# A decoder layer on one core: SwiGLU gate and up products as seven block products, the down product in a stage of its own

## The chip, the cores and the metric

The kernel runs on one core of one Trainium2 chip. The metric is the device time of one execution in microseconds (us). Engines are called as in the profile: PE (TensorE), with PEld its weight loads, DVE (VectorE), ACT (ScalarE), POOL (GpSimd), SP (SyncE, which only issues DMAs here).

## The reference, cut to what matters

One layer of a decoder: 1024 tokens of width 1024, float32. Two gated mixers, a cross attention to 256 memory tokens, and a SwiGLU feed-forward of width 2816, each with a normalisation ahead and a residual add behind. The part in question is the last:

```python
def _swiglu(n, w_gate, w_up, w_down):
    return (jax.nn.silu(n @ w_gate) * (n @ w_up)) @ w_down
...
        h = h + _swiglu(_rmsnorm(h, g_ffn[l]), w_ffn_gate[l], w_ffn_up[l], w_ffn_down[l])
    return _rmsnorm(h, g_final)
```

## The kernel before

Activations lie transposed: features on the 128 partitions, 1024 tokens along a row, so a tensor of width 1024 is eight tiles of 128x1024. Every large product is done in three passes over float32 values that are split in a rounded part ("hi") and the rest ("lo"): hi by hi, lo by hi, hi by lo. One matmul takes a 128x128 block of weights and 512 tokens (a "half"); all these come from one line, L387 in `passes`.

Weights come as a stream of 276 tiles of 128x1024 (512 KB) in `weights`. SP loads them in turn into the two buffers of `stage` (L338); POOL makes `w_hi` (L350, two instructions of 128x512) and `w_lo` (L355, four of 128x256) in `split`; PE waits for `w_split` and tells with `w_begun` that it has begun a tile. A tile's buffers are written again when PE has begun the tile after it.

The stages at the end of the kernel, in PE's order:

- The output product of the cross attention ("OM", W_OM on): four weight tiles, each with four banks of PSUM of 12 matmuls. DVE adds each bank to the residual `h` (`add_product`, L1410). As soon as a tile of `h` has both halves, `next_operand` runs on ACT (n_hi = h times gain L1028, square L1031) and on DVE (n_lo L1417, sum of squares into `rms` L1421).
- Feed-forward, gate and up (`wide`): for each of 22 feature tiles a gate tile and an up tile, two halves each, 8 blocks of K by 3 passes = 24 matmuls in a bank. The operands are `n_hi` and `n_lo`, whose mean square goes through PE (`mean`, L408) during the first tile. DVE reads a bank and multiplies by `rms` (`half_out`, L1508), ACT applies Silu (L1081), DVE multiplies gate by up (L1516), ACT rounds (`a_hi`, L1083) and DVE takes the rest (`a_lo`, L1518).
- Down (`down`): for each pair of feature tiles, 16 banks of 6 matmuls on `a_hi` and `a_lo`. It is worked inside the loop, behind the first gate tile of the next pair, 11 pairs in all; the last pair stands behind the loop (`last_down`). DVE adds every bank to `h`.
- The tail: final normalisation (ACT L1108 squares, POOL L368 sums, DVE L1550 scales) and the stores.

Order and waits are written by hand: each engine has its own program, with loops (`Fori`), and waits on semaphores.

The tensors `stage`, `w_hi`, `w_lo`, `n_hi`, `n_lo` stand first in on-chip memory, each a multiple of 8 KB long per partition. Behind them stand some small ones (`gain` 160 bytes, `rope_c` and `r_col` 8, `stat` 112), and behind those all others, such as `m_hi`, `qm_hi`, `a_hi`.

## Time and profile before

| | |
|---|---|
| median of 3 runs | 1899.01 us (1897.57 to 1899.85) |
| the profiled execution | 1899.36 us, of which the span of the trace 1897.6 us |
| granted TensorE clock, mean | 0.975 of full speed |
| busy: PE / DVE / POOL / ACT | 94% / 52% / 37% / 33% of the span |
| instructions | 24569, of them 8610 matmuls |

Busy time counts overlapping matmuls, so a busy PE is no proof of PE at its best pace; the distance between the starts of matmuls is the better measure. The feed-forward lies in the last 750 us.

### The profile page before, as it was taken

How to read it: one execution, taken by the hardware profiler on the slowest of the kernel's cores; microseconds unless marked ns; L12 is line 12 of the kernel's file. 1: busy time of each engine (PE TensorE's matmuls, PEld its weight loads, DVE VectorE, ACT ScalarE, POOL GpSimd, SP SyncE). 2: the span in 40 equal slices, each digit the busy share in tenths (PEclk: the TensorE clock that was granted, in tenths of full speed). 3: DMA queues.
4: the chain of work that ended last, by engine and by line, in shares of the span. 5: the costliest groups of instructions: out<-in, count | busy, mean ns of one | idle time of the engine just before them, and what ended most of it. 6: DMA issues, size and time to landing. Idle time of an engine off the chain costs nothing.

```text
span 1897.6 us, 24569 instructions
## 1 busy us (share of the span) xinstructions
PE 1782.4 (94%) x8610; PEld 1446.1 (76%) x8610; DVE 994.6 (52%) x1490; ACT 629.1 (33%) x1009; POOL 709.6 (37%) x848
## 2 busy tenths in 40 slices
PE   3799999999999999789999899999999999999996
PEld 3677777777778777668887777888888888888884
DVE  7446894688469757865434553332332333333236
ACT  4215773576367557743113332000000000000003
POOL 5632223132313122134553034444434434443435
PEclk8899999999999999889999999999999999999998
DMA  5311112112111211263212011111111111111112
GB/s 191 123 46 46 31 51 64 46 39 66 49 46 38 77 40 50 90 221 133 78 55 78 12 34 45 52 48 44 44 55 44 45 55 44 44 49 50 44 44 89
DMA packets 42201, 118.59 MB, mean 62 GB/s; under 512 B 5136, under 2 KB 13584, under 8 KB 42000
## 3 DMA queue, kind: packets, MB, share of 16 engines
q1 hardware_dynamic: 21312, 75.66, 11.8%
q10 hardware_dynamic: 20816, 41.95, 6.7%
q8 instruction: 46, 0.75, 0.2%
q14 instruction: 27, 0.22, 0.0%
HBM read 97.67 MB, written 18.87 MB: 61 GB/s over the span
## 4 chain that ended last, share of the span: by engine, by line
PE 83%; DVE 7%; ACT 3%; issue 3%; DVEq 0%; ACTq 0%; POOL 0%; DMA 0%; POOLq 0%
PE ps L387 70%; PE ps L533 4%; PE ps L496 3%; PE ps L510 3%; DVE e_row L1310 1%; DVE e_row L1307 1%; DVE pt L1340 1%; DVE h L1550 1%; DVE rows L1319 1%; ACT n_hi L1028 1%; PE ps L529 1%; DVE rms L1421 1%; DVE h L1410 0%; ACT p_m L1054 0%; PE ps L663 0%
## 5 line engine op out<-in xcount | busy, mean ns | idle before, releaser
L350 POOL TENSOR_SCALAR w_hi<-w_stage 128x512 fp32r<-128x512 f32 x276 | 200.9, 745 | 1159.3 <-issue 622.5
L355 POOL TENSOR_TENSOR w_lo<-w_stage,w_hi 128x256 fp32r<-128x256 f32 x552 | 487.4, 913 | 11.5
L387 PE MATMUL ps<-n_hi,w_hi 128*128 128x512 f32 x1536 | 395.2, 398 | 11.0 <-DVE n_lo L1260 7.0
L387 PE MATMUL ps<-n_lo,w_hi 128*128 128x512 f32 x1536 | 386.2, 392 | 0.0
L387 PE MATMUL ps<-n_hi,w_lo 128*128 128x512 f32 x1536 | 385.7, 391 | 0.0
L387 PEld LDWEIGHTS ps<-n_hi,w_hi 128*128 128x128 f32 x1536 | 288.1, 190 | 74.0 <-issue 12.0
L387 PEld LDWEIGHTS ps<-n_lo,w_hi 128*128 128x128 f32 x1536 | 287.3, 188 | 59.8 <-issue 0.2
L387 PEld LDWEIGHTS ps<-n_hi,w_lo 128*128 128x128 f32 x1536 | 286.0, 188 | 58.6
L1410 DVE TENSOR_TENSOR h<-ps,h 128x512 f32<-128x512 f32 (+1 forms) x192 | 132.1, 691 | 160.0 <-PE ps L387 160.0
L1083 ACT ACTIVATE a_hi<-u_f 128x1024 fp32r<-128x1024 f32 x22 | 23.4, 1065 | 466.3 <-DVE u_f L1516 466.3
L1508 DVE TENSOR_TENSOR u_f<-ps,rms 128x512 f32<-128x512 f32 x44 | 30.4, 692 | 205.3 <-PE ps L387 205.3
L910 ACT ACTIVATE pt<-ps 128x256 fp32r<-128x256 f32 (+3 forms) x96 | 77.9, 811 | 134.0 <-PE ps L510 133.9
L1340 DVE TENSOR_TENSOR pt<-ps,pt 128x256 fp32r<-128x256 f32 (+3 forms) x96 | 91.9, 957 | 49.7 <-ACT pt L910 45.6
L387 PE MATMUL ps<-a_hi,w_hi 128*128 128x512 f32 x352 | 111.3, 395 | 1.7 <-DVE a_lo L1518 1.7
L387 PE MATMUL ps<-a_hi,w_lo 128*128 128x512 f32 x352 | 111.7, 396 | 0.0
L387 PE MATMUL ps<-a_lo,w_hi 128*128 128x512 f32 x352 | 111.5, 396 | 0.0
L1217 DVE TENSOR_TENSOR raw<-ps,rms 128x512 f32<-128x512 f32 x80 | 54.8, 685 | 92.5 <-PE ps L387 92.5
L1508 DVE TENSOR_TENSOR g_f<-ps,rms 128x512 f32<-128x512 f32 x44 | 30.3, 691 | 123.1 <-PE ps L387 120.9
L1081 ACT ACTIVATE g_f<-g_f 128x1024 f32<-128x1024 f32 x22 | 23.3, 1061 | 177.8 <-DVE g_f L1508 177.7
L510 PE MATMUL ps<-ident,rows 128*128 128x128 f32 x576 | 81.4, 279 | 0.0
L387 PEld LDWEIGHTS ps<-a_hi,w_hi 128*128 128x128 f32 x352 | 66.1, 188 | 18.8 <-DVE a_lo L1518 2.1
L387 PEld LDWEIGHTS ps<-a_hi,w_lo 128*128 128x128 f32 x352 | 66.1, 188 | 16.2
(175 smaller groups left out, 2212.2 us busy)
## 6 DMA issues: line engine op xcount, KB each, us to landing
w_stage<-weights_in SPq DMA_DIRECT2D x138, 512.0 KB, 3.3
gates_scratch<-raw ACTq DMA_DIRECT2D x16, 512.0 KB, 2.8
o_scratch<-o_sum ACTq DMA_DIRECT2D x64, 64.0 KB, 2.1
n_lo<-o_scratch ACTq DMA_DIRECT2D x8, 512.0 KB, 3.8
g_a<-gates_scratch ACTq DMA_DIRECT2D x8, 512.0 KB, 3.7
g_b<-gates_scratch ACTq DMA_DIRECT2D x8, 512.0 KB, 4.5
h<-x_t_in ACTq DMA_DIRECT2D x8, 512.0 KB, 7.5
out_t<-h ACTq DMA_DIRECT2D x16, 256.0 KB, 2.1
```

The source lines that it names most:

```text
L350: ins = pool.tensor_scalar(w_hi[:, b, at], stage[:, b, at], 1.0, 1.0, ALU.mult, ALU.mult)
L355: ins = pool.tensor_tensor(w_lo[:, b, at], stage[:, b, at], w_hi[:, b, at].bitcast(F32), ALU.subtract)
L387: ins = pe.matmul(bank, w[:, b, c:c + P], mv(k), start=(first and n == 0), stop=(last and n == total - 1))
L496: ins = pe.matmul(ps[:, 2 + h, 0:width(s)], a[hs, blk(qb)], b[hs, at], start=(n == 0), stop=(n == 2 and not diagonal))
L510: ins = pe.transpose(ps_t[:, h, n, :], rows[:, s % 4, h, blk(n)], ident[:])
L533: ins = pe.matmul(ps[:, r, blk(h, 2 * P)], v_of[m][:, c + kb, h, :, :].rearrange("p a d -> p (a d)"), pt[:, h, kb, :, :].rearrange("p a q ...
L910: act.activation(pt[:, :, 0:n, 0, :], ps_t[:, :, 0:n, :], ACT.Copy).then_inc(pt_hi_s, 1)
L1083: act.activation(a_hi[:, f, :], u_f[:, f, :], ACT.Copy).then_inc(a_hi_s, 1)
L1217: dve.tensor_tensor(raw[:, RAW[name], blk(half, HALF)], ps[:, half, :], rms[:, blk(half, HALF)], ALU.mult).then_inc(bank_free, 1)
L1340: dve.tensor_tensor(pt[:, :, 0:n, 1, :], ps_t[:, :, 0:n, :], pt[:, :, 0:n, 0, :].bitcast(F32), ALU.subtract).then_inc(pt_lo_s, 1)
L1410: dve.tensor_tensor(hj, ps[:, bank + half, :], hj, ALU.add).then_inc(bank_free, 1)
L1508: dve.tensor_tensor(dst[:, blk(half, HALF)], ps[:, bank + half, :], rms[:, blk(half, HALF)], ALU.mult).then_inc(bank_free, 1)
```

## The change

The gate and up products are taken in 2x2 blocks: the token halves and the halves of K (features 0 to 3 and 4 to 7 of eight) on the side of the activations (A11, A12, A21, A22), the halves of K and two feature tiles on the side of the weights (B11 to B22). Seven products of blocks, with four sums on each side (S1 to S4, T1 to T4) and sums of results, stand in place of the eight. A "group" is the gate or the up product of two feature tiles; there are 22 groups, each 7 products of 12 matmuls.

- The left operands (seven, with hi and lo for four blocks of K) are made once, during OM: DVE makes the sums from `h`, ACT rounds, DVE takes the rest. The first two blocks of K lie in `n_hi` and `n_lo`, so do A11 and A22 of the fourth; the others lie in new tensors `left_2`, `left_a`, `left_b` at the far end. All of this is now in pieces of 128x512, four steps n of OM, one for each weight tile.
- The right operands: DVE makes T1 to T4 for the next group, ACT rounds all seven into a ring of four slots (in place of POOL), POOL takes only the rest (two instructions of 128x256 each).
- PE leaves banks open: a bank is read by ACT (`snapshot`) after one product and PE goes on adding to it. DVE puts the four blocks of the result together from snapshots and banks.
- The hidden tiles (gate times up) are stored to memory by SP, 1 MB for a pair, and loaded again in the down stage, where they are split by ACT and DVE in `n_hi` and `n_lo`. Down's 11 pairs follow one another at the end.

The core of the diff:

```diff
+LEFT = {"A11": 0, "S1": 1, "S2": 2, "S4": 3, "S3": 4, "A12": 5, "A22": 6}
+SPLIT_AS = ("A22", "S1", "A11", "S2", "S3", "A12", "S4")
+RIGHT = ("B11", "T1", "T2", "B22", "T3", "B21", "T4")
+SLOT = (0, 1, 2, 3, 0, 1, 2)
+MADE = {"T3": 1, "T1": 2, "T2": 3, "T4": 4}
+GROUPS = 2 * FPAIRS
...
+        def left(name, k):
+            r = LEFT[name]
+            if k < 2:
+                return n_hi[:, r, blk(k, HALF)], n_lo[:, r, blk(k, HALF)]
+            if k == 2:
+                return left_2[:, r, 0, :], left_2[:, r, 1, :]
+            if name in ("A11", "A22"):
+                at = blk(name == "A22", HALF)
+                return n_hi[:, KT - 1, at], n_lo[:, KT - 1, at]
+            t, r = (left_a, int(name[1]) - 1) if name in ("S1", "S2", "S3") else (left_b, int(name == "S4"))
+            return t[:, r, 0, :], t[:, r, 1, :]
...
+            for g in range(GROUPS):
+                tile = W_FF + 2 * g
+                split_before = W_FF + 7 * (g - 1)
+                sp.wait_ge(w_split, split_before + 4 if g else W_FF - 1)
+                sp.dma_start(stage[:, 0, 0:HALF], weights[tile][:, 0:HALF]).then_inc(b11_in, 16)
+                if g == 0:
+                    sp.dma_start(stage[:, 0, HALF:], weights[tile][:, HALF:]).then_inc(b21_in, 16)
+                    sp.wait_ge(w_split, W_FF)
+                sp.dma_start(stage[:, 1, :], weights[tile + 1]).then_inc(f2_in, 16)
+                if g % 2 and g > 1:
+                    store_hidden(g // 2 - 1)
+                if g:
+                    sp.wait_ge(w_split, split_before + 6)
+                    sp.wait_ge(t_made, 4 * g)
+                    sp.dma_start(stage[:, 0, HALF:], weights[tile][:, HALF:]).then_inc(b21_in, 16)
+            sp.wait_ge(w_begun, W_DOWN - 7 + 3)
+            load_hidden(0)
+            sp.wait_ge(t_made, 4 * GROUPS)
+            load_down(0)
+            load_down(1)
...
+            with pool.Fori(0, GROUPS) as g:
+                for pos, name in enumerate(RIGHT):
+                    b, c = ring(pos)
+                    pool.wait_ge(w_rounded, g * 7 + (W_FF + pos + 1))
+                    for part in range(2):
+                        at = slice(c + part * 2 * P, c + (part + 1) * 2 * P)
+                        ins = pool.tensor_tensor(w_lo[:, b, at], right(name)[:, blk(part, 2 * P)],
+                                                 w_hi[:, b, at].bitcast(F32), ALU.subtract)
+                    ins.then_inc(w_split, 1)
...
+            def seven(g, up, first=False):
+                y, z, x = (3, 4, 5) if up else (0, 1, 2)
+                for pos, (bank, opening, closing) in enumerate((
+                        (y, True, False), (z, True, False), (y, False, False), (z, False, True),
+                        (y, False, False), (x, True, True), (y, False, True))):
+                    name = ("A11", "S1", "S2", "S4", "S3", "A12", "A22")[pos]
+                    b, c = ring(pos)
+                    pe.wait_ge(w_split, g * 7 + (W_FF + pos + 1))
+                    if pos == 0 and not first:
+                        pe.wait_ge(c_read, g * 3 - 3)
+                    if pos in (2, 3, 4, 6):
+                        pe.wait_ge(snapped, g * 4 + {2: 1, 3: 2, 4: 3, 6: 4}[pos])
+                    for p, w in enumerate((w_hi, w_hi, w_lo)):
+                        for k in range(4):
+                            if first and not up and k in (0, 3) and p < 2:
+                                made = 7 * k + SPLIT_AS.index(name) + 1 if k else 21
+                                pe.wait_ge((nhi_ready, nlo_ready)[p], 2 * KT + made)
+                            ins = pe.matmul(ps[:, bank, :], w[:, b, c + k * P:c + (k + 1) * P], left(name, k)[p == 1],
+                                            start=(opening and p == 0 and k == 0), stop=(closing and p == 2 and k == 3), skip_group_check=True)
+                            if p == 0 and k == 0:
+                                ins.then_inc(w_begun, 1)
+                    ins.then_inc(prod, 1)
...
+            for p in range(2):
+                pe.wait_ge(a_lo_s, 2 * p + 2)
+                down(W_DOWN + 2 * p, p, B_FF + 2 * KT * p, p == 0)
...
+            def right_hi(g, pos, first=False):
+                name = RIGHT[pos]
+                if first and pos < 4:
+                    act.wait_ge(w_begun, W_FF + pos // 2)
+                elif pos < 3:
+                    act.wait_ge(w_begun, g * 7 + (W_FF - 7 + pos + 4 + 2))
+                elif pos == 3:
+                    act.wait_ge(w_begun, g * 7 + (W_FF - 7 + 3 + 2))
+                else:
+                    act.wait_ge(w_begun, g * 7 + (W_FF + pos - 4 + 2))
...
+                act.activation(w_hi[:, b, c:c + HALF], right(name), ACT.Copy).then_inc(w_rounded, 1)
...
+            def group(g, up, first=False, ending=False):
+                begun = first and not up
+                snapshot(g, up, 0, 0, begun)
+                right_hi(g, 4)
+                snapshot(g, up, 1, 1)
+                right_hi(g, 5)
+                snapshot(g, up, 2, 2)
+                right_hi(g, 6)
+                snapshot(g, up, 3, 4)
+                if ending:
+                    return
+                right_hi(g + 1, 0)
+                if begun:
+                    factors(3)
+                    act.preload_act_table(ACT.Silu)
+                right_hi(g + 1, 1)
+                if not up:
+                    silu(g, 1)
+                right_hi(g + 1, 2)
+                right_hi(g + 1, 3)
+                if not up:
+                    silu(g, 0)
...
+            for q in range(2):
+                square(3, q)
+            right_hi(0, 2, True)
+            for q in range(2, 4):
+                square(3, q)
+            right_hi(0, 3, True)
...
+            for n in range(4):
+                grow(n, 0)
+                if n:
+                    add_square(n - 1, 0)
+                    add_square(n - 1, 1)
+                grow(n, 1)
+                dve.wait_ge(n21_s, n + 1)
+                left_sum(n, "S1", 1, "S3", ALU.add)
+                if n == 3:
+                    for name in ("T3", "T1", "T2"):
+                        right_sum(0, name, True)
+                grow(n, 2)
+                dve.wait_ge(sum_s, 4 * n + 1)
+                left_sum(n, "S2", 2, "S1", ALU.subtract)
+                left_sum(n, "S3", 2, "S3", ALU.subtract)
+                if n:
+                    add_square(n - 1, 2)
+                    add_square(n - 1, 3)
+                left_lo(n, "A22", 1)
+                left_lo(n, "S1")
+                grow(n, 3)
+                dve.wait_ge(sum_s, 4 * n + 2)
+                left_sum(n, "S4", 3, "S2", ALU.add)
+                left_lo(n, "A11", 2)
+                left_lo(n, "S2")
+                left_lo(n, "S3")
+                left_lo(n, "A12", 3)
+                left_lo(n, "S4")
+            right_sum(0, "T4", True)
+            for c in range(4):
+                add_square(3, c)
...
+            def group(g, up, first=False, ending=False):
+                y, z, x = (3, 4, 5) if up else (0, 1, 2)
+                dst = u_f if up else g_f
+                def factor(f, half):
+                    return g_f[:, f, blk(half, HALF)] if up else rms[:, blk(half, HALF)]
+                def scale(f, half):
+                    part = dst[:, f, blk(half, HALF)]
+                    return dve.tensor_tensor(part, part, factor(f, half), ALU.mult)
+                if up:
+                    for f in (1, 0):
+                        dve.wait_ge(silu_ready, g + (1 - f))
+                        dve.tensor_tensor(g_f[:, f, :], g_f[:, f, :], rms[:], ALU.mult).then_inc(gr_made, 1)
+                    if not first:
+                        dve.wait_ge(a_out, g * 16 - 16)
+                dve.wait_ge(prod, g * 7 + 4)
+                dve.wait_ge(snapped, g * 4 + 3)
+                dve.tensor_tensor(dst[:, 1, 0:HALF], snap[:, 2, :], ps[:, z, :], ALU.add).then_inc(c_read, 1)
+                if not ending:
+                    right_sum(g + 1, "T3")
+                    right_sum(g + 1, "T1")
+                dve.wait_ge(snapped, g * 4 + 4)
+                dve.tensor_tensor(dst[:, 1, HALF:], snap[:, 3, :], snap[:, 1, :], ALU.add).then_inc(c22_made, 1)
+                if not ending:
+                    right_sum(g + 1, "T2")
+                if first and not up:
+                    raw_factors(3)
+                    dve.wait_ge(rms_ready, 3)
+                if up:
+                    dve.wait_ge(gr_made, g + 1)
+                dve.wait_ge(c_read, g * 3 + 1)
+                scale(1, 0)
+                dve.wait_ge(c22_made, g + 1)
+                scale(1, 1).then_inc(tile1_made, 1)
+                dve.wait_ge(prod, g * 7 + 6)
+                dve.tensor_tensor(dst[:, 0, 0:HALF], snap[:, 0, :], ps[:, x, :], ALU.add).then_inc(c_read, 1)
+                if ending:
+                    for f in range(2):
+                        hidden_lo(0, 0, f)
+                else:
+                    right_sum(g + 1, "T4")
+                dve.wait_ge(c_read, g * 3 + 2)
+                scale(0, 0)
+                dve.wait_ge(prod, g * 7 + 7)
+                dve.tensor_tensor(dst[:, 0, HALF:], ps[:, y, :], factor(0, 1), ALU.mult).then_inc(c_read, 1)
```

In what is left out, `left_sum`, `left_lo` and `add_square` are one DVE instruction of 128x512 each, `snapshot` and `square` one of ACT; `down` and `last_down` take `n_hi` and `n_lo` in place of `a_hi` and `a_lo`, and DVE's `hidden_lo` for the next pair stands behind the adds of n = 4 and 5.

## Rows read from the trace of the kernel before

**Rows 1.** The page: busy time and share of each engine; the chain by engine.
```profile
PE 1782.4 (94%) x8610; PEld 1446.1 (76%) x8610; DVE 994.6 (52%) x1490; ACT 629.1 (33%) x1009; POOL 709.6 (37%) x848
PE 83%; DVE 7%; ACT 3%; issue 3%; DVEq 0%; ACTq 0%; POOL 0%; DMA 0%; POOLq 0%
```

**Rows 2.** Chain in order of time: start us, us, what.
```profile
1160.63 692.44 PE ps L387 x3024
1853.09 0.70 DVE u_f L1508
...
1857.57 14.27 PE ps L387 x60
```

**Rows 3.** Stretch from the loop to its end: busy us (instructions), clock, DMA share.
```profile
1203.00:1853.00 650.00, 650.00 (x2839) 532.55 (x2838) 211.84 (x276) 41.45 (x39) 275.11 (x354) 1.00 0.14 47
```

**Rows 4.** PE in order of time (start us, us): operands n, a and m.
```profile
1237.37 1.98 PE L387 MATMUL ps<-n_hi,w_hi 128*128 128x512 f32 x8
...
1242.81 1.98 PE L387 MATMUL ps<-n_hi,w_hi 128*128 128x512 f32 x8
1208.26 0.62 PE L387 MATMUL ps<-a_hi,w_hi 128*128 128x512 f32 x2
...
1209.66 0.62 PE L387 MATMUL ps<-a_hi,w_hi 128*128 128x512 f32 x2
985.93 2.02 PE L387 MATMUL ps<-m_hi,w_hi 128*128 128x512 f32 x8
987.79 2.03 PE L387 MATMUL ps<-m_lo,w_hi 128*128 128x512 f32 x8
```

**Rows 5.** All engines in order of time, from OM to the first gate tile.
```profile
1100.10 1.91 PE L387 MATMUL ps<-qm_hi,w_hi 128*128 128x512 f32 x4 [1.35 <-DVE qm_lo L1487]
1104.54 1.09 PE L387 MATMUL ps<-qm_hi,w_hi 128*128 128x512 f32 x4
1104.86 0.69 DVE L1410 TENSOR_TENSOR h<-ps,h 128x512 f32 x1 [4.16 <-PE ps L387]
1146.54 1.78 PE L387 MATMUL ps<-n_hi,w_hi 128*128 128x512 f32 x7
1149.29 0.50 PE L387 MATMUL ps<-n_hi,w_hi 128*128 128x512 f32 x1 [0.96 <-ACT n_hi L1028]
```

**Rows 6.** DVE by line: 128x512 on two inputs of on-chip memory; on PSUM.
```profile
L1397 DVE TENSOR_TENSOR y_a<-y_a,y_b x16: 691/692/1085, 829.6 to 908.6; 128x512 f32<-128x512 f32 x16
L1401 DVE TENSOR_TENSOR m_lo<-y_a,m_hi 128x512 f32 x16 | 12.7, 796 | 15.2 <-ACT m_hi L1005 15.2
L1508 DVE TENSOR_TENSOR u_f<-ps,rms 128x512 f32<-128x512 f32 x44 | 30.4, 692 | 205.3 <-PE ps L387 205.3
```

**Rows 7.** The tail in order of time.
```profile
1860.08 15.69 POOL L368 TENSOR_TENSOR rms<-rms,sq 128x512 f32<-128x512 f32 x11 [0.59 <-ACT sq L1108]
1871.67 1.02 PE L408 MATMUL ps<-rms,mean_w 128*128 128x512 f32 x2
1879.50 8.09 DVE L1550 SCALAR_TENSOR_TENSOR h<-h,gain,rms 128x512 f32<-128x512 f32 x8 [0.46 <-ACT rms L1097]
1883.78 2.08 PE L408 MATMUL ps<-rms,mean_w 128*128 128x512 f32 x2 [5.47 <-POOL rms L368]
1889.55 5.39 DVE L1550 SCALAR_TENSOR_TENSOR h<-h,gain,rms 128x512 f32<-128x512 f32 x8 [1.36 <-ACT rms L1097]
```

**Rows 8.** ACT by line: 128x512 from on-chip memory and PSUM; 128x1024 Silu.
```profile
L1005 ACT ACTIVATE m_hi<-y_a 128x512 f32 x12 | 7.6, 632 | 43.0 <-DVE y_a L1397 43.0
L1062 ACT ACTIVATE pm_hi<-ps 128x512 fp32r<-128x512 f32 x16 | 9.5, 596 | 0.5 <-PE ps L650 0.5
L1081 ACT ACTIVATE g_f<-g_f 128x1024 f32<-128x1024 f32 x22 | 23.3, 1061 | 177.8 <-DVE g_f L1508 177.7
```

**Rows 9.** POOL: `split` beside few and beside many DVE instructions; extremes.
```profile
1204.60 1.20 POOL L350 TENSOR_SCALAR w_hi<-w_stage 128x512 fp32r<-128x512 f32 x2 [4.84 <-PE ps L387]
1205.89 2.84 POOL L355 TENSOR_TENSOR w_lo<-w_stage,w_hi 128x256 fp32r<-128x256 f32 x4
1125.98 4.80 POOL L355 TENSOR_TENSOR w_lo<-w_stage,w_hi 128x256 fp32r<-128x256 f32 x4
L355 POOL TENSOR_TENSOR w_lo<-w_stage,w_hi x552: 712/740/1791, 13.9 to 1858.8; 128x256 fp32r<-128x256 f32 x184
```

**Rows 10.** DMA issues: KB each, median us to landing.
```profile
w_stage<-weights_in SPq DMA_DIRECT2D x58, 512.0 KB, 3.2
```

More of the change, by code:

```diff
@@ L684, in _ @@
                         last.then_inc(bank_full, 1)
-            def wide(b, start, ring_at, wait=None):
-                for half in range(2):
-                    pe.wait_ge(bank_free, start + (half - 3))
-                    if wait and half == 0:
-                        lead, last = product(ps[:, ring_at + half, :], b, half, (0, 2, 1), wait=wait)
-                    else:
-                        lead, last = product(ps[:, ring_at + half, :], b, half)
-                    if half == 0:
-                        lead.then_inc(w_begun, 1)
-                    last.then_inc(bank_full, 1)
@@ L699, in down @@
-            def down(tile, buffer, start, ring_at):
+            def seven(g, up, first=False):
[20 more added lines that the diff above has]
+                    ins.then_inc(prod, 1)
+                    if first and not up and pos == 4:
+                        mean(4 * KT + 1)
@@ L700, in down @@
+            seven(0, False, True)
+            seven(1, True, True)
+            with pe.Fori(1, FPAIRS) as i:
+                seven(i * 2, False)
+                seven(i * 2 + 1, True)
+            def down(tile, buffer, start, seam=False):
                 for n in range(KT):
+                    b = n // 4
                     if n % 4 == 0:
-                        begin_tile(tile + (n // 4 + 1))
-                    b = (n // 4 + buffer) % 2
+                        begin_tile(tile + (b + 1))
@@ L735, in last_down @@
                 return passes(ps[:, c % 4, :], lambda k: (n // 4, k * HALF + (n % 4) * P),
-                              lambda k: a_hi[:, k, blk(half, HALF)], lambda k: a_lo[:, k, blk(half, HALF)],
+                              lambda k: n_hi[:, k, blk(half, HALF)], lambda k: n_lo[:, k, blk(half, HALF)],
                               (0, 1, 2), ks, 0 in ks, last)
@@ L758, in _ @@
                 if c == KT + 3:
[L759 to L760 removed]
+                    mean(5 * KT + 1, (0,))
+            mean(6 * KT + 1, (1,))
         @block.scalar
@@ new lines, in snapshot, with silu @@
+            def snapshot(g, up, which, pos, first=False):
+                act.wait_ge(prod, g * 7 + (pos + 1))
+                if which == 0 and not first:
+                    act.wait_ge(c_read, g * 3 - 1)
+                bank = 3 * up + (which == 1)
+                act.activation(snap[:, which, :], ps[:, bank, :], ACT.Copy).then_inc(snapped, 1)
+            def silu(g, f):
+                if f:
+                    act.wait_ge(tile1_made, g + 1)
+                else:
+                    act.wait_ge(c_read, g * 3 + 3)
+                act.activation(g_f[:, f, :], g_f[:, f, :], ACT.Silu).then_inc(silu_ready, 1)
@@ L1091, in _ @@
+            group(0, False, True)
+            group(1, True, True)
+            with act.Fori(1, FPAIRS - 1) as i:
+                group(i * 2, False)
+                group(i * 2 + 1, True)
+            group(GROUPS - 2, False)
+            group(GROUPS - 1, True, ending=True)
+            for p in range(FPAIRS):
+                hidden_hi(p)
             act.preload_act_table_set("natural_log_exp_and_others")
@@ L1593, in down @@
         return list(tiles(rows, HALF))
-    out += [g[0], u[0], g[1], u[1]]
-    for p in range(1, FPAIRS):
-        out += [g[2 * p], *down(p - 1), u[2 * p], g[2 * p + 1], u[2 * p + 1]]
-    out += down(FPAIRS - 1)
+    for p in range(FPAIRS):
+        out += [g[2 * p], g[2 * p + 1], u[2 * p], u[2 * p + 1]]
+    for p in range(FPAIRS):
+        out += down(p)
     return np.stack(out)
```

265 lines of the change are left out of this document (182 added, 83 removed).

## The prediction

> **What bounds the kernel now.** I read the page first. PE is busy 94% of the span and holds 83% of the chain of waits; no other engine holds over 7% [rows 1]. Then the chain in order of time: from 1160.63 it is one piece of 692.44 us of matmuls, then 4.5 us over DVE and ACT, in which PE idles 1.7 us for the last hidden tile, then matmuls again [rows 2]. The window 1203 to 1853 says the same: PE 650 of 650 us at the full granted clock (2.4 GHz), DVE busy 33%, POOL 42%, ACT 6%, DMA 14% [rows 3]. So in the feed-forward a matmul less is time less, as long as the three other engines keep up.
>
> What a matmul costs I take from starts. On `n_hi`/`n_lo`: 1242.81 - 1237.37 = 5.44 us for 24, 0.2267 us each. On `a_hi`/`a_lo`: 1.40 us for 6, 0.2333. On `m_hi`: 1.86 for 8, 0.2333 [rows 4]. The dearer ones are just the operands that stand behind the small tensors; the length of a pass is not the reason, as m runs passes of eight too. I give new operands in that region 0.2333, those in `n_hi`/`n_lo` 0.2267.
>
> Check: 2112 gate and up matmuls (22 tiles x 2 x 2 x 24) x 0.2267 = 478.8 us, 960 of down ahead of the last pair x 0.2333 = 224.0, mean 1.5, stall 1.4 ahead of the last n_hi: 705.7. The trace has 706.4 from 1146.54 [rows 5] to 1852.9, the start of the last pair.
>
> **The matmuls.** Gate and up: 22 groups x 84 = 1848. Of a group's 28 pairs of product and block of K, 16 (k = 0 and 1, and k = 3 of A11 and A22) lie in `n_hi`: 48 x 0.2267 + 36 x 0.2333 = 19.28 us a group, 2.75 a product, 424.2 in all, against 478.8: -54.6. Down: 1056 matmuls move to `n_hi`: 1056 x 0.0067 = -7.0. Sum -61.6. Bounds: all new operands cheap, 5.3 us less; all of them and down dear, 10 us more.
>
> **OM becomes DVE's.** Before, a step of OM (one weight tile) gave DVE 4 adds and some work on 128x1024. Now each step has 4 reads of PSUM at 0.69, and 15 instructions of 128x512 on on-chip memory (4 left sums, 7 low parts, 4 adds of squares). Such an instruction takes 0.69 alone (L1397 median), 0.80 to 0.84 as a mean beside POOL [rows 6], and 8.09/8 = 1.01 with POOL busy throughout against 5.39/8 = 0.67 without [rows 7]. POOL works here 4 x 6.1 = 24 us of some 65 [rows 9], so I take 0.80. A step: 2.8 + 12.0, plus 1.3 in which DVE waits behind its first read for ACT's copy and square (2 x 0.63 [rows 8]), plus 0.4 for its waits on itself: 16.5 us. PE needs 48 x 0.2333 = 11.2. DVE falls behind.
> From DVE's first read (1104.86 [rows 5]) as zero: step 0 ends at 15.3 (no squares to add; banks set its first half), steps 1 and 2 at 48.3. In step 3 the low part of A11 comes after 4 reads, 14 instructions (T3, T1, T2 among them) and the waits, 15.7: at 64.0. There PE stands inside its first product, which could have begun at 41.7 (1146.54). It ends that at 65.1. Its third product waits for a snapshot that stands in ACT's queue behind two squares and the rounding of B22, and the second square waits for DVE's add of a square: four low parts, T4, the add (6 x 0.80), then 4 x 0.63 on ACT: 71.4. Unhindered it would begin at 41.7 + 5.5 = 47.2. Cost 24.2 us; the old stall of 1.4 goes. The same sum with 0.69 gives 17.5, with 1.01 it gives 37: the ends. The clock: behind an idle of 5.47 us two matmuls of the mean took 2.08 us in place of 1.02 [rows 7], half the clock (1.2 GHz); and the first eight of OM took twice their time [rows 5], 1.7 us. Part of that hides in the wait for the snapshot: +1.0 (0 to 1.7).
>
> **A group in steady state.** Time from the group's start, PE's products at 0, 2.75 and so on; each wait against the moment it is needed.
> Right operand 0 of the next group: its slot is free at 13.8, ACT does the snapshot due at 14.0 first (0.60), rounds by 15.3, POOL's two instructions take 1.4 to 2.4 (2.84/4 and 4.80/4 each [rows 9]): 17.7 at worst, needed at 19.3. The others follow with 1.9 and more in hand. POOL in all: 14 x 1.20 = 16.8 of 19.3 at worst.
> Snapshots: a bank is full, 0.2 later ACT reads it (0.60), and PE wants it a product (2.75) later: 1.9 in hand.
> DVE: 8.5 us in a gate group, 11 in an up group. ACT: 11 x 0.62 + 2 x 1.06 = 8.9. The tightest place is ACT's queue from gate to up: the snapshot stands behind Silu of the first tile, and Silu behind DVE's last read. At 1.01 an instruction DVE ends that at 22.05, Silu at 23.2, the snapshot at 23.8; needed at 24.8. In hand 1.0.
> DMA: a group's weights are asked for at 5.6 and land (3.2 us [rows 10]) by 9.5; T3 reads them at 12. Stores and loads of hidden tiles add 22 MB over 650 us where the engines are 14% busy [rows 3]; SP meets its waits in that order with some 5 us to spare.
> I cost the steady state at nothing. If that cover goes, each us is 11 or 22 us.
>
> **The seam.** PE's last group ends at 19.3. POOL can begin to split the first down tile only when the last product has begun (16.6), and needs 4.1 to 6.1 us [rows 9]: ready at 20.7 to 22.7. Stall 1.4 to 3.4, I take 2.5. The hidden tile's low part is done by 20.6 and hides in it. Down runs 21.8 us a pair; DVE needs 16 x 0.69 + 2 x 1.3 = 13.7, the split of two tiles 12.2: nothing.
>
> **The tail.** The last pair now finds its hidden tile ready: -1.7 [rows 2]. But POOL's sums of squares (15.69/11 = 1.43 each [rows 7]) were just level with PE's banks of 1.40 when PE came to the mean of the first half. PE now arrives at 16.3 us from the pair's start, the eighth sum at 6.1 + 11.4 = 17.5: +1.2. Behind it nothing changes.
>
> **Sum.** -61.6 - 1.4 + 24.2 + 1.0 + 2.5 - 1.7 + 1.2 = -35.8. The profiled execution took 1899.4 (span 1897.6 and 1.8 around it), 0.35 above the median of the runs: 1863.6, say 1864.
>
> **The rivals.**
> A, the preparation keeps up. DVE at 0.69 throughout and the new tensors at 0.2267: -6.7 - 5.3, 1852. For it: the median of L1397 is 0.692. Against: DVE is now busy without a break, so it must meet POOL's 24 us, and a step is 14.9 us even at 0.69, against PE's 11.2. Chance 0.12.
> B, DVE is stopped by whole POOL instructions. If every 128x512 of DVE took 0.69 + 0.71 = 1.40 while POOL works, then the six such instructions behind the fourth snapshot of a gate group end 2.3 us later than at 1.01; 1.0 is in hand: 1.3 late x 11 = 14 us. In OM 24/1.40 = 17 instructions lose 0.71 each, 12 us where I counted 6.6: +5. Together 1883. POOL itself would still fit: 14 x 0.71 + 8.0 = 18 of 19.3. For it: a maximum of 1.085, and POOL's 1.20 in place of 0.71. Against: DVE's mean beside POOL of 1.01, not 1.40. Chance 0.16.
> The Trainium skill, page "SBUF — State Buffer", section "SBUF: two separate sides", has the rule behind B: DVE instructions with two inputs in SBUF and GpSimd instructions that read SBUF take a shared port pair as an exclusive lock for a whole instruction. Trace and rule agree that both sides lengthen; the 1.01 says that DVE does not wait for a full one each time.
> C, slower than before: POOL becomes the bound. Its 14 subtractions a group hold PE as soon as one takes over 19.28/14 = 1.38 us, and eat the whole gain over (19.28 + 35.8/22)/14 = 1.49. The longest in the trace is 1.79: 25.1 us a group, +127, 1991. For it: POOL's pace has varied 0.71 to 1.79 [rows 9], and ACT, DVE and POOL must hand on every slot in turn. Against: the densest stretch shows 1.20. Chance 0.09.
>
> **How the numbers follow.** Forecast 1864 with 0.63, its own range 1853 to 1877; A 1852 with 0.12, B 1883 with 0.16, C with 0.09. The range 1850 to 1885 leaves out C and a little of B and A, under 2 in 10. A difference of 0.2% (3.8 us) is about what this kernel's measurement tells from none. Faster: forecast, A and B but for 0.02 on the far side of B (35.8/22 = 1.6 us a group lost would be no change): 0.89. Within: 0.02. Slower: C, 0.09.
>
> **What would show it.** Starts of products 2.75 us apart in the loop, 19.3 a group, and 0.2267 against 0.2333 by operand: the first term. A wait of PE of some 20 us in all between 1146 and 1180, on DVE's low part first, then on ACT's snapshot, with a half clock in it: OM. One stall of 2 to 3 us on POOL at the seam, near 1597. No idle of PE in between. Wrong it would be if groups came 20 us apart or more, with waits on ACT's snapshot (B) or on POOL (C), or if PE passed from OM to the first group within 10 us.

## The result, and the profile after

The changed kernel takes 1866.99 us in the median of four runs (1866.63 to 1870.18), the kernel before 1899.03 (1897.57 to 1899.85): a ratio of 0.9835 (in brackets, here and below, the 95% interval: [0.9821, 0.985]). The forecast was 1864 with 1850 to 1885. The profiled execution took 1866.63, 32.7 less than the profiled one of before; its span is 32.8 less.

The page: busy time by engine and the chain by engine, against [rows 1].

```profile
PE 1733.5 (93%) x8346; PEld 1401.5 (75%) x8346; DVE 1143.5 (61%) x1688; ACT 777.6 (42%) x1283; POOL 766.9 (41%) x892
PE 79%; DVE 6%; issue 5%; ACT 3%; POOL 2%; ACTq 0%; DMA 0%; DVEq 0%; POOLq 0%
```

PE is busy 49 us less and still holds the chain. DVE and ACT each do some 149 us more. The chain now has 2% of POOL: that is the stretch between OM and the third product ("the prologue" below) and the tail, with a little of the seam between the last product and down.

PE in order of time, from output-multiply (OM) to the third product, against [rows 5].

```profile
1101.03 1.96 PE L492 MATMUL ps<-qm_hi,w_hi 128*128 128x512 f32 x4 [1.35 <-DVE qm_lo L1707]
...
1138.61 1.21 PE L492 MATMUL ps<-qm_hi,w_hi 128*128 128x512 f32 x4 [1.52 <-DVE h L1723]
...
1161.25 1.22 PE L811 MATMUL ps<-n_hi,w_hi 128*128 128x512 f32 x2 [9.94 <-POOL w_lo L461]
...
1167.47 0.80 PE L811 MATMUL ps<-n_lo,w_hi 128*128 128x512 f32 x1 [2.86 <-DVE n_lo L1745]
...
1169.77 1.05 PE L811 MATMUL ps<-n_hi,w_hi 128*128 128x512 f32 x2
...
1172.75 0.45 PE L811 MATMUL ps<-left_a,w_hi 128*128 128x512 f32 x1
...
1174.00 0.71 PE L811 MATMUL ps<-n_hi,w_hi 128*128 128x512 f32 x2
```

The third product starts 72.97 us after OM. Before, OM took 1146.54 - 1100.10 = 46.44 up to its successor [rows 5]; with two products of 2.75 that is 51.94. The prologue costs 21.0. Worked out from the starts of matmuls, that is some 3.7 inside OM itself (PE waits four times, 2.6 in all, for DVE to read a bank), 10.1 between OM and the first product, 3.1 for the wait at 1167.47, and 4.2 by which the first two products' matmuls ran slower than in the loop, at half the clock (0.43 apart, not 0.232). OM started 0.9 later than before, in a stage that isn't changed.

The other engines in that stretch: what holds those waits.

```profile
1156.95 0.68 DVE L1755 TENSOR_TENSOR t_raw<-w_stage 128x512 f32<-128x512 f32 x1
1157.55 0.68 DVE L1758 TENSOR_TENSOR w_stage<-w_stage 128x512 f32<-128x512 f32 x1
1158.16 0.68 DVE L1761 SCALAR_TENSOR_TENSOR t_raw<-t_raw,w_stage 128x512 f32<-128x512 f32 x1
1158.64 1.13 ACT L1207 ACTIVATE w_hi<-w_stage 128x512 fp32r<-128x512 f32 x2
1159.34 4.14 POOL L461 TENSOR_TENSOR w_lo<-w_stage,w_hi 128x256 fp32r<-128x256 f32 x4 [27.79 <-ACT w_hi L1207]
...
1161.67 2.36 DVE L1730 TENSOR_TENSOR rms<-rms,sq 128x512 f32<-128x512 f32 x2
...
1173.32 0.58 ACT L1256 ACTIVATE snap<-ps 128x512 f32<-128x512 f32 x1
```

ACT rounds B11 only at 1158.64, behind its work on the left factor; POOL, idle for 27.79 us, then needs 1.9 for the low part, and PE starts at 1161.25. DVE's starts lie 0.60 apart where POOL is idle, less than the listed 0.68, and two instructions beside POOL take 2.36. The first snapshot ends at 1173.90, 0.1 ahead of the third product. So PE hardly waited for it, but only because the second product, at half clock for most of its length, was through no earlier: at the full clock PE would have stood there until about the same moment (an estimate).

The loop: PE in order of time inside a product of A22, whose 12 operands are 9 from `n_hi`/`n_lo` and 3 from `left`; then, against [rows 3], the stretch as a whole (PE, weight loads, DVE, ACT, POOL).

```profile
1304.26 0.62 PE L811 MATMUL ps<-n_hi,w_hi 128*128 128x512 f32 x2
1304.72 0.40 PE L811 MATMUL ps<-left,w_hi 128*128 128x512 f32 x1
1304.95 0.39 PE L811 MATMUL ps<-n_hi,w_hi 128*128 128x512 f32 x1
...
1307.04 0.63 PE L811 MATMUL ps<-n_hi,w_hi 128*128 128x512 f32 x2
```

```profile
1195.60:1596.80 401.20, 401.20 (x1730) 324.81 (x1731) 200.49 (x245) 151.09 (x247) 249.37 (x288) 1.00 0.24 86
```

One product takes 1307.04 - 1304.26 = 2.78. Over the stretch 144 products took 1596.56 - 1195.60 = 400.96, 2.784 each, with no idle of PE and the full granted clock.

The seam and the first of down; then the first half's mean and the last wait of the tail, against [rows 7].

```profile
1599.11 0.39 PE L811 MATMUL ps<-n_hi,w_lo 128*128 128x512 f32 x1
1603.53 1.19 PE L492 MATMUL ps<-n_hi,w_hi 128*128 128x512 f32 x2 [4.03 <-issue]
1604.52 1.05 PE L492 MATMUL ps<-n_lo,w_hi 128*128 128x512 f32 x2
...
1606.23 0.69 PE L492 MATMUL ps<-n_hi,w_hi 128*128 128x512 f32 x2
...
1609.06 0.62 PE L492 MATMUL ps<-n_hi,w_hi 128*128 128x512 f32 x2
1609.51 0.61 PE L492 MATMUL ps<-n_lo,w_hi 128*128 128x512 f32 x2
1609.97 0.62 PE L492 MATMUL ps<-n_hi,w_lo 128*128 128x512 f32 x2
1610.42 0.62 PE L492 MATMUL ps<-n_hi,w_hi 128*128 128x512 f32 x2
...
1839.12 1.13 PE L513 MATMUL ps<-rms,mean_w 128*128 128x512 f32 x2
...
1851.03 2.08 PE L513 MATMUL ps<-rms,mean_w 128*128 128x512 f32 x2 [5.30 <-POOL rms L473]
```

POOL's last low part came at 1599.37 + 4.06 = 1603.43. The first six matmuls of down then took 2.70 and not 1.36: half the clock (1.2 GHz) after an idle of 4.0. In down six take 1610.42 - 1609.06 = 1.36, 0.2267 each, as forecast.

### The profile page after: what moved, and what is told of

Its sections match the earlier page's. It is cut to its first block, busy times and chain, and to the rows that moved or that the text cites. A ratio compares the mean times of both kernels' runs of the same rounds, so it can differ in the third digit from the quotient of the medians.

```text
span 1864.8 us, 24982 instructions
## 1 busy us (share of the span) xinstructions
PE 1733.5 (93%) x8346; PEld 1401.5 (75%) x8346; DVE 1143.5 (61%) x1688; ACT 777.6 (42%) x1283; POOL 766.9 (41%) x892
## 4 chain that ended last, share of the span: by engine, by line
PE 79%; DVE 6%; issue 5%; ACT 3%; POOL 2%; ACTq 0%; DMA 0%; DVEq 0%; POOLq 0%
PE ps L492 45%; PE ps L811 22%; PE ps L638 4%; PE ps L601 3%; PE ps L615 3%; POOL w_lo L461 1%; DVE e_row L1530 1%; POOL rms L473 1%; DVE pt L1560 1%; DVE e_row L1527 1%; DVE h L1889 1%; DVE rows L1539 1%; PE ps L634 1%; POOL w_lo L446 0%; ACT p_m L1173 0%
## 5 line engine op out<-in xcount | busy, mean ns | idle before, releaser
L441 POOL TENSOR_SCALAR w_hi<-w_stage 128x512 fp32r<-128x512 f32 x188 | 128.3, 700 | 884.5 <-issue 457.9
L446 POOL TENSOR_TENSOR w_lo<-w_stage,w_hi 128x256 fp32r<-128x256 f32 x376 | 346.7, 952 | 7.9
L492 PE MATMUL ps<-n_hi,w_hi 128*128 128x512 f32 x1184 | 329.9, 400 | 14.2 <-DVE n_lo L1480 7.1
L492 PE MATMUL ps<-n_lo,w_hi 128*128 128x512 f32 x1184 | 321.8, 393 | 0.0
L492 PE MATMUL ps<-n_hi,w_lo 128*128 128x512 f32 x1184 | 321.2, 392 | 0.0
L492 PEld LDWEIGHTS ps<-n_hi,w_hi 128*128 128x128 f32 x1184 | 222.1, 191 | 62.7 <-issue 16.5
L492 PEld LDWEIGHTS ps<-n_lo,w_hi 128*128 128x128 f32 x1184 | 221.9, 189 | 46.0 <-issue 0.2
L492 PEld LDWEIGHTS ps<-n_hi,w_lo 128*128 128x128 f32 x1184 | 220.2, 188 | 44.9
L461 POOL TENSOR_TENSOR w_lo<-w_stage,w_hi 128x256 fp32r<-128x256 f32 x176 | 163.7, 950 | 146.9 <-ACT w_hi L1207 146.9
L1256 ACT ACTIVATE snap<-ps 128x512 f32<-128x512 f32 x88 | 52.6, 598 | 183.5 <-PE ps L811 183.4
L461 POOL TENSOR_TENSOR w_lo<-t_raw,w_hi 128x256 fp32r<-128x256 f32 x132 | 108.8, 845 | 41.9 <-ACT w_hi L1207 41.6
L811 PE MATMUL ps<-n_hi,w_hi 128*128 128x512 f32 x352 | 115.3, 399 | 10.1 <-POOL w_lo L461 10.1
L811 PE MATMUL ps<-left,w_hi 128*128 128x512 f32 x308 | 122.6, 398 | 0.0
L811 PE MATMUL ps<-n_lo,w_hi 128*128 128x512 f32 x352 | 114.8, 397 | 2.9 <-DVE n_lo L1745 2.9
L811 PE MATMUL ps<-n_hi,w_lo 128*128 128x512 f32 x352 | 114.5, 396 | 0.0
```

Source lines behind the costliest of these rows:

```text
L441: ins = pool.tensor_scalar(w_hi[:, b, at], stage[:, b, at], 1.0, 1.0, ALU.mult, ALU.mult)
L446: ins = pool.tensor_tensor(w_lo[:, b, at], stage[:, b, at], w_hi[:, b, at].bitcast(F32), ALU.subtract)
L461: ins = pool.tensor_tensor(w_lo[:, b, at], right(name)[:, blk(part, 2 * P)], w_hi[:, b, at].bitcast(F32), ALU.subtract)
L492: ins = pe.matmul(bank, w[:, b, c:c + P], mv(k), start=(first and n == 0), stop=(last and n == total - 1))
L811: ins = pe.matmul(ps[:, bank, :], w[:, b, c + k * P:c + (k + 1) * P], left(name, k)[p == 1], start=(opening and p == 0 and k == 0), stop=( ...
```

## The experiments

Three groups of four ran on one chip each, with the kernel before beside them (1898.00, 1899.11 and 1899.29), so kernels are compared by their ratios to it. For the prologue I use the time from OM's start to the third product. Its size depends on something no edit touches: where the first eight matmuls of OM ran at half clock it is 1.6 longer (72.97 after; 71.40 in experiment 4, the run with the traffic cut, whose prologue is the same code).

**1. Alignment: is the dearer operand a matter of its address?** 32 bytes ahead of the tensors in question, in both kernels.

```diff
+            ("pad_0", [P, 8], F32), ("m_hi", [P, KT, T], F32R), ...
...
+            ("pad_1", [P, 8], F32), ("qm_hi", [P, MH, T], F32R), ...
...
+(_, left_b, g_f, u_f, snap, left_2, t_raw) = phase(("pad_2", [P, 8], F32),
```

> The changed kernel, with all tensors of the last stages moved by 32 bytes, so that m_hi, qm_hi and the left operands behind stat start at a multiple of 64 bytes as n_hi does; nothing else is changed. Theory (the start address of the moving operand sets 0.2267 or 0.2333 us a matmul): products of the groups go from 2.784 to 2.72 us, 154 x 0.064 = 10 us less, and m_hi and OM gain 384 x 0.0067 + 192 x 0.0067 = 3.9 us: ratio to before about 0.976, 1853 us. Rival (the mix of operands or the groups' own waits cost the extra time, not the address): products stay at 2.78 us, the time within 2 us of 1867.

> The kernel before, with the same move by 32 bytes of m_hi, qm_hi, a_hi and what lies behind them. Theory of the address: 1056 matmuls of down, 384 on m_hi and 192 of OM go from 0.2333 to 0.2267: 1632 x 0.0067 = 10.9 us less, 1888 us, ratio 0.994; then 7 us of the change's gain came from where down's operands lie, and not from the seven products. Rival: no change.

After with the move: 1863.02, 0.9818 [0.9804, 0.9831]; 1728 matmuls of the loop took 399.8 us where after took 401.1 (2.776 a product): 1.3 less, where the theory wants 0.064 x 144 = 9.2. The ratio's interval overlaps after's. Before with the move: 1898.19, 1.0 [0.9991, 1.0009], `a_hi` still 1.40 for 6, `m_hi` 1.87 for 8. This alignment is not what makes an operand dear; the theory fell.

**2. Which term is the operand's: `n_hi` in place of the others.** In before only down's operand, in after all left operands (so both multiply other data than the reference).

```diff
-    lambda k: a_hi[:, k, blk(half, HALF)], lambda k: a_lo[:, k, blk(half, HALF)],
+    lambda k: n_hi[:, k, blk(half, HALF)], lambda k: n_lo[:, k, blk(half, HALF)],
```

> The kernel before, whose down product reads n_hi and n_lo in place of a_hi and a_lo (so down multiplies other data; number, order and waits stay). Theory, the operand's tensor sets the matmul's spacing: a bank takes 1.36 us and not 1.40, 1056 matmuls x 0.0067 = 7.0 us less: 1891 to 1892, ratio 0.9963, which is the prediction's term for down. Rival, the 0.2333 of before comes from down's being woven between gate and up tiles: 1899, ratio 1.000, 1.40 a bank.

```diff
-        def left(name, k):
+        def left(name, k, near=False):
...
+            if near:
+                return n_hi[:, r, blk(k % 2, HALF)], n_lo[:, r, blk(k % 2, HALF)]
...
-                            ins = pe.matmul(ps[:, bank, :], ..., left(name, k)[p == 1],
+                            ins = pe.matmul(ps[:, bank, :], ..., left(name, k, True)[p == 1],
```

> The kernel after, whose seven products read all moving operands from n_hi and n_lo (so the sums of the left factor aren't multiplied; number, order, banks and waits stay). Theory, the tensor sets the spacing and every change of tensor counts: 0.2267 a matmul, 2.72 us a product, 154 x 0.064 = 10 us less than the kernel after: 1857, ratio 0.978. Rival, something else in the seven products' stage (the other engines' work beside it, the banks, the pattern) sets 0.232: still 2.78, 1867, ratio 0.983.

PE in order of time in down of the first (against [rows 4], `a_hi`), then in the products of the second.

```profile
1206.46 0.62 PE L387 MATMUL ps<-n_hi,w_hi 128*128 128x512 f32 x2
...
1207.82 0.62 PE L387 MATMUL ps<-n_hi,w_hi 128*128 128x512 f32 x2
```

```profile
1301.25 1.07 PE L813 MATMUL ps<-n_hi,w_hi 128*128 128x512 f32 x4
...
1303.97 1.07 PE L813 MATMUL ps<-n_hi,w_hi 128*128 128x512 f32 x4
```

Six take 1.36, and a product 2.72. The times: 1893.35, 0.9972 [0.9962, 0.9983], so down's term is -5.3 (-7.2 to -3.2), which holds the -7.0 that was summed; and 1855.80, 0.9778 [0.9763, 0.9794], which is 0.0057 x 1899 = 10.8 us below after's. With the same number, order, banks and waits, the tensors that the matmuls read set their spacing. It is not the values in them: down multiplies the same hidden tiles, up to rounding, in after as in before, and takes 1.36 for six from `n_hi` and 1.40 from `a_hi`. Nor is it a change of tensor as such: the second kernel still changes between `n_hi` and `n_lo` every four matmuls, at no cost.

**3. Or is it the work beside it?** Every matmul of the seven products issued twice in a row (the sums are doubled), so that the other engines' work is half as dense.

```diff
-                            ins = pe.matmul(ps[:, bank, :], w[:, b, ...], left(name, k)[p == 1],
...
+                            for again in range(2):
+                                ins = pe.matmul(ps[:, bank, :], w[:, b, ...], left(name, k)[p == 1],
```

> The kernel after, whose seven products issue every matmul twice in a row (so each sum is doubled); the other engines do the same work in twice the time. Theory, the work of DVE, ACT and POOL beside the products makes the spacing 0.232 in place of 0.229: with it half as dense, 0.2305, a product of 24 takes 5.53. Rival, the spacing belongs to the operands and their changes: repeating the same operand halves the changes, n_hi ones at 0.2267, the mean at 0.229 or 0.232 as for each operand alone. Either way 154 x 2.77 = 426 us more, about 2293; the spacing of pairs by tensor is what tells.

```profile
1299.90 1.09 PE L812 MATMUL ps<-n_hi,w_hi 128*128 128x512 f32 x4
1300.82 0.63 PE L812 MATMUL ps<-left,w_hi 128*128 128x512 f32 x2
1301.29 0.64 PE L812 MATMUL ps<-left_b,w_hi 128*128 128x512 f32 x2
...
1305.50 1.09 PE L812 MATMUL ps<-n_hi,w_hi 128*128 128x512 f32 x4
```

The loop in the chain of waits (start us, us, what).

```profile
1194.07 831.54 PE ps L812 x3576
```

2287.47. The double product shown takes 1305.50 - 1299.90 = 5.60; those of A11 and A22, with more operands in `n_hi`, take 5.54. Over the loop 3576 matmuls took 831.54, 0.2325 each, against 0.2320 in after (2.784/12): no cheaper with the other engines' work half as dense, so the work beside isn't the cause. Those from `left` stand 0.235 apart; four from `n_hi` between two others take 0.92 where they take 0.907 in a row of their own. So `n_hi` matmuls inside a pass lose about 0.01 by their neighbours; in after a pair takes 0.463 and not 0.453. That it is the change between `n_hi` and the new tensors is read from these spacings alone, and was not tried by itself.

**4. The hidden tiles' traffic.** Stores and loads of 8 of 1024 columns (most of the hidden data is left out).

```diff
-                sp.dma_start(a_d[2 * p + 1], u_f[:, 1, :]).then_inc(a_out, 16)
+                sp.dma_start(a_d[2 * p + 1][:, 0:8], u_f[:, 1, 0:8]).then_inc(a_out, 16)
...
```

> The kernel after, whose stores and loads of the hidden tiles move 8 of 1024 columns of each tile (so most of the hidden tiles' data is left out); the transfers, their waits and the order stay. My theory: the tiles' way through memory costs nothing, since in the kernel after no engine waits for it except at the seam, where the waits are for the split of weights and the low part: same time as the kernel after within 0.3%, 1866 to 1868 (ratio 0.983 to 0.985), and a product stays at 2.78 us. Rival, the transfers take ports or queues from the weights' loads and so make the slower pace of 2.784 in place of 2.754 us a product: 1862 (0.981), product 2.75.

1864.76, 0.9823 [0.981, 0.9836]. From the third product to down's first matmul 429.5 us in both (after: 1603.53 - 1174.00), so the traffic costs nothing there. The median lies 1.2 below the range expected; the profile has OM's first matmuls at full clock, which is worth 1.6.

**5. POOL in the loop.** Each low part of a right operand made twice.

```diff
                         ins = pool.tensor_tensor(w_lo[:, b, at], right(name)[:, blk(part, 2 * P)], ...
+                    ins.then_inc(w_twice, 1)
+                    pool.wait_ge(w_twice, g * 7 + (pos + 1))
+                    for part in range(2):
...
+                        ins = pool.tensor_tensor(w_lo[:, b, at], right(name)[:, blk(part, 2 * P)], ...
```

> The kernel after, in which POOL makes the low parts of every right operand twice, 28 subtractions a group and not 14, from the same data. In the loop of after POOL takes 0.86 us for one (249 us for some 290). Rival C's mechanism (POOL becomes the bound when its work in a group exceeds PE's 19.5 us): 28 x 0.86 = 24.1 and about 1 for the hand-over, 25 us a group, with waits of PE on w_lo: 22 x 5.5 = 121 us more, 1988, ratio 1.047. If POOL is not on the path even then (it speeds up, or runs ahead): no change, 1867.

The stretch 1200 to 1600 by engine (PE, weight loads, DVE, ACT, POOL), and what PE waited for from 1200 to 1700.

```profile
1200.00:1600.00 400.00, 339.48 (x1356) 252.53 (x1355) 185.23 (x192) 118.78 (x194) 391.05 (x456) 0.98 0.18 63
```

```profile
PE ps L817 <- POOL w_lo L467: 54.8, 42, 2.2
PE ps L817 <- DVE g_f L1861: 12.6, 8, 1.6
```

1977.79, 1.0416 [1.0396, 1.0436]: 110.8 more, 5.0 a group, 24.5 in all, where 25 was expected, and POOL busy 98%. Rival C's mechanism exists; the one point tried, beyond its bound, fits its rule. POOL at 0.86 an instruction simply stays under the bound (14 x 0.86 = 12 of 19.5).

**6. DVE's load in OM.** POOL adds the first 12 squares in DVE's place.

```diff
-                if n:
-                    add_square(n - 1, 0)
-                    add_square(n - 1, 1)
...
+            for q in range(12):
+                part = rms[:, blk(1 - q % 4 // 2, HALF)]
...
+                pool.tensor_tensor(part, part, sq[:, blk(q % 2, HALF)], ALU.add).then_inc(summed, 1)
```

> The changed kernel, with the first 12 of the 16 adds of squares in OM done by POOL, which stands idle there for 27 us, in place of DVE. Theory (DVE's queue holds up the left operands): DVE loses 12 instructions of 0.6 to 1.0 us and three waits of 1.3 us ahead of the low part of A11, 10 to 14 us; PE comes to its third product 8 to 12 us earlier than now (72 us behind the start of OM), time 1856 to 1859. Rival 1 (PE is held by POOL's low part of B11, which ACT's order delays to 1161): at most 4 us less. Rival 2 (POOL and DVE now block each other): under 3 us less.

```profile
1152.31 3.21 POOL L459 TENSOR_TENSOR rms<-rms,sq 128x512 f32<-128x512 f32 x2
1152.64 1.75 DVE L1764 TENSOR_TENSOR w_stage<-w_stage 128x512 f32<-128x512 f32 x1
...
1163.40 0.79 PE L817 MATMUL ps<-n_lo,w_hi 128*128 128x512 f32 x1 [0.45 <-DVE n_lo L1751]
...
1169.25 0.58 ACT L1262 ACTIVATE snap<-ps 128x512 f32<-128x512 f32 x1
...
1169.93 0.69 PE L817 MATMUL ps<-n_hi,w_hi 128*128 128x512 f32 x2 [1.29 <-issue]
```

1865.42, 0.9835 [0.9821, 0.9848], third product at 72.79 (after 72.97). Twelve instructions less on DVE bought nothing, as Rival 2 had it: DVE's took 1.75 beside POOL's adds, and the third product waited 1.29 for the snapshot in ACT's queue (1169.25 + 0.58 = 1169.83).

**7. The order in the prologue, the clock, the seam.** Four kernels. The seam: POOL splits the first tile of down in halves, each as soon as its slot is free.

```diff
+            for part in range(2):
+                pool.wait_ge(w_begun, W_DOWN - 1 + part)
+                at = blk(part, HALF)
+                pool.tensor_scalar(w_hi[:, 0, at], stage[:, 0, at], 1.0, 1.0, ALU.mult, ALU.mult).then_inc(w_rounded, 1)
...
```

> The changed kernel, with POOL splitting the first down tile in two halves, the first half as soon as the sixth product of the last group is done with its slot, in place of the whole tile once the seventh has begun. Theory (the 4.2 us stall between the last group and down is POOL's split): the stall falls to some 1.5 us, 2 to 3 us less, 1864.5. Rival (the hidden tile's low part on DVE ends it): the low part is there at 1600.4, 1 us behind the last product, so the stall would be 1.1 at least; if load or ACT are late, no change.

```profile
1595.08 0.62 PE L822 MATMUL ps<-n_hi,w_hi 128*128 128x512 f32 x2
...
1596.83 2.88 DVE L1816 TENSOR_TENSOR n_lo<-n_lo,n_hi 128x1024 fp32r<-128x1024 f32 x2
...
1600.38 0.70 PE L503 MATMUL ps<-n_hi,w_hi 128*128 128x512 f32 x2 [2.36 <-DVE n_lo L1816]
```

1862.10, 0.9816 [0.9803, 0.983]. From the last product's start to down 5.30 and not 6.97: 1.7 less, where 2 to 3 was expected, since then DVE's low part of the hidden tile is what comes last (the rival, with 2.4 of stall).

The prologue, with three moves at once: B11 rounded at the start of OM's last step, two squares behind the first snapshot, DVE's second read of a step ahead of its adds (PE then waits by itself for the banks to be free).

```diff
             for n in range(4):
+                if n == 3:
+                    right_hi(0, 0, True)
...
-                    right_hi(0, 0, True)
...
                 snapshot(g, up, 0, 0, begun)
+                if begun:
+                    for q in range(2, 4):
+                        square(3, q)
...
                 grow(n, 0)
+                grow(n, 1)
                 if n:
                     add_square(n - 1, 0)
                     add_square(n - 1, 1)
-                grow(n, 1)
...
```

> The kernel after with three moves in the prologue: ScalarE rounds B11 at the start of output-multiply step 3 and not near its end, its last two squares come behind the first snapshot, and VectorE reads the second bank of a step ahead of the adds of squares. Theory that ScalarE's order sets the first three products: low half of B11's weights about 4 us earlier, first product starts at 1157 to 1159 and not 1161.25, third about 2 to 3 us earlier than 73.0 us from the start of output multiply: 1864 (0.982). Rival, the length of VectorE's sequence sets the third product: first product earlier but its last part and the third still wait for VectorE's low parts, third at 72.5 to 73: 1866 to 1867 (0.9833).

```profile
1148.38 0.70 PE L813 MATMUL ps<-n_hi,w_hi 128*128 128x512 f32 x2 [2.57 <-issue]
...
1154.96 0.80 PE L813 MATMUL ps<-n_hi,w_hi 128*128 128x512 f32 x1 [5.65 <-ACT n_hi L1229]
...
1161.30 0.79 PE L813 MATMUL ps<-n_lo,w_hi 128*128 128x512 f32 x1 [4.26 <-DVE n_lo L1749]
...
1166.88 0.63 PE L813 MATMUL ps<-n_hi,w_hi 128*128 128x512 f32 x2
```

1863.12, 0.9815 [0.9801, 0.9828]. The first product starts far earlier, at 49.72, and waits inside itself; the third starts at 1166.88 - 1098.66 = 68.22, 3.2 less than 71.40 (both with OM's first matmuls at full clock). The moves are not told apart by a run, but the trace divides them: 2.2 of the 3.2 stand at DVE's last low part already (1161.30 - 1098.66 = 62.64 against 64.87 in experiment 4), and DVE's waits for squares alone fell from 1.31 to 0.71 in each of three steps, 1.8 in all. So most of the gain came with DVE's own order, and about 1 from ACT's, by the squares that no longer stand ahead of the snapshot. B11, rounded early, only let PE start sooner and wait inside the product. The wait that is left is DVE's.

Then, as well, matmuls into an unused bank ahead of the first product:

```diff
+            pe.wait_ge(nhi_ready, 2 * KT + 14)
+            for _ in range(38):
+                pe.matmul(ps[:, 7, :], w_hi[:, 1, 0:P], n_hi[:, 0, 0:HALF], start=True, stop=True)
             seven(0, False, True)
```

> As the one before, and TensorE runs 38 matmuls into an unused bank after output multiply, so that it isn't idle while it waits. Theory: the first two products at 0.23 us a matmul and not 0.43; the first ends some 2 us earlier, the second too, and with them the first snapshot; the third product starts 1 to 2.5 us earlier than in the one before: 1862 (0.981). Rival, the third product waits for VectorE's low part in any case, and the clock before it is worth nothing: same as the one before within 0.5 us; if the extra matmuls run past the release of the first product, slower by up to 1 us.

```profile
1165.08 0.80 PE L813 MATMUL ps<-n_lo,w_hi 128*128 128x512 f32 x1 [5.17 <-DVE n_lo L1752]
```

1864.68, 0.982 [0.9807, 0.9834]: third product at 70.16, with OM's first matmuls at half clock, so 68.5 on the other scale. No gain: the 38 matmuls kept the clock, but then PE waited 5.17 for DVE's low part inside the first product, and nine matmuls behind it were at half clock again. Keeping the clock up to that last wait was not tried; in the run before, the 17 matmuls from the wait to the third product took 5.58 where 17 x 0.232 = 3.9, so at most 1.6 us hang on it (an estimate).

And all of these with the seam in halves:

> As the one before, with the seam's weights split in halves ahead of the loop: the two savings add up if they are on the path: 1.7 us less than the one before, about 1860 (0.980). Rival, none (it is the sum of two); if it is no better than the run with the seam in halves alone, the moves in the prologue are worth nothing.

1862.08, 0.981 [0.9796, 0.9823], no better in the median than the seam alone (1862.10), though its profile has both savings (third product at 68.52; down 2.4 us late and not 4.0). So that the two savings add up is not shown by the times. The runs of one kernel spread by up to 5.6 us (1862.71 to 1868.27 in experiment 6): a gain of 2 or 3 us is read from the traces here, not from the times.

## Why the prediction was right, and where it was not

The mechanism was right stage by stage: fewer matmuls give the gain, OM's preparation gives a third of it back, one stall at the seam, no idle in the loop. Within the prologue the order of the waits was half right. The sum (-35.8) against the trace (-32.8):

| Term | predicted | measured | difference |
|---|---|---|---|
| Gate and up, 154 products | 2.754 each | 2.784 each | +4.6 |
| Down on `n_hi` | 0.2267 | 0.2267 | 0 |
| Prologue and its clock | 25.2 | 21.0 | -4.2 |
| Stage ahead of OM | 0 | 0.9 | +0.9 |
| Seam, stall | 2.5 | 4.2 | +1.7 |
| Seam, half clock | not counted | 1.3 | +1.3 |
| Tail, last pair to the end | -0.5 | -1.9 | -1.4 |

The differences add to +2.9: -32.9 against -32.8. That the sum is so close is partly luck: errors of +8.5 and -5.6 cancel for the most part. The tail: the last pair began at 1822.58 in after and at 1852.89 before, so it took 42.2 and 44.7 to the span's end; 0.6 of the 2.5 is the cheaper operand (96 matmuls x 0.0067), counted in its own term.

- **Gate and up.** "`n_hi` costs 0.2267, an operand of the other region 0.2333" was right for runs of one tensor [rows 4] and too low where they alternate within a pass of four: by these two prices a product of A11 or A22, with 9 cheap operands of 12, would take 2.74 and the others 2.76, and all take 2.78 to 2.79. The rows used had eight in a row of one tensor; the sum needed a row with a change in it. Experiment 2 shows the 10 us that hang on the tensor. The bound "all of them and down dear, 10 us more" is added up wrong (1056 x 0.0067 twice is 14); nothing else hangs on it.
- **OM.** DVE's step was near enough by two errors that cancel: its instructions stand 0.60 apart when POOL is idle, not 0.69, and 1.1 to 1.2 each beside POOL, where I spread 0.80 over all. Counted from DVE's first read (1106.10), the low part of A11 released PE at 61.4 (predicted 64.0) and the third product began at 67.9 (predicted 71.4). I let the first product start at 41.7 and stand inside; in fact it could not start until 1161.25, since ACT rounds B11 behind its left factor work. I followed ACT's queue for the snapshot and not for the first right operand. This miss cost little, since DVE's low part came at 1167.47 anyway: with B11 early (experiment 7) PE only waits inside the product. The snapshot was the last in ACT's queue as predicted, but PE did not stand idle for it: the half clock, which I had put at +1.0, took 4.2 in the first two products and filled that time. It became the last wait as soon as DVE was relieved (experiment 6).
- **The steady state** at nothing held: POOL 62% busy, no wait of PE, and experiment 4 shows the stores and loads free.
- **The seam.** I took 2.5 out of 1.4 to 3.4, and 4.2 lies outside. POOL began 0.6 behind the last product's start, and its tile took 6.3 (1597.12 to 1603.43), over the slow end of [rows 9]; DVE's 128x1024 subtraction ran beside it (that it is the cause is not shown). The idle drops the clock as it did in [rows 7], which I had counted in the prologue only.
- **The tail.** +1.2 for POOL's sums did not come: the mean of the first half ran 16.5 us after the last pair's start, about the 18.8 of before less its old stall of 1.7 and 0.5 for the operand. POOL's first sum began 5.1 behind that start (1827.69), and not 6.1 as I had it.
- **Rivals.** A: the prologue's 21.0 lies halfway between its 17.5 and my 24.2; its cheap operands were wrong. B: beside POOL's 128x256 instructions one of DVE takes 1.1 to 1.2 from start to start, more than the 1.01 of [rows 7] and less than B's 1.40; beside POOL's longer adds of 128x512 in experiment 6 they start 1.68 apart, where 0.60 does without. The Trainium skill, page "SBUF — State Buffer", section "SBUF: two separate sides", has an exclusive lock for a whole instruction. The trace agrees in part: in experiment 6 the two engines go in step, one DVE instruction to one of POOL's, but 1.68 is less than the 1.3 and 0.6 that they take alone. B's price in the loop did not come: PE waited there for neither ACT nor DVE. C: experiment 5.

## What to carry to other kernels

When a matmul is taken out of a stage that PE bounds, price the remaining ones from rows with the same alternation of operands, and place the new operands where the cheap ones are if there is room. Preparation that all must pass before the first product is paid once but whole: follow each engine's queue up to the first item that is needed, and move that item ahead of the work that is only needed later, on the engine that comes last first of all. Taking work off the engine that is last helps only if it doesn't go to one that makes it slower.
